# FFN up-projection of a streaming encoder layer: 16 block products per weight tile against seven, with stored weight operands

## The reference

```python
D_MODEL = 1024; SEQ = 2048; DEC_SEQ = 64; D_FF = 2816; FFN_CONV = 3

def causal_dwconv(x, prev, w, b):          # one row for each position
    xp = jnp.concatenate([prev.astype(x.dtype), x], axis=1)
    y = b.astype(x.dtype) + w[0] * xp[:, 0:L]
    for j in range(1, k_width):
        y = y + w[j] * xp[:, j:j + L]
    return y, xp[:, L:]

# in trunk_layer, x being (positions, 1024) and ffn_w_in (1024, 5632)
up, ffn_conv_state = causal_dwconv(x @ ffn_w_in, ffn_conv_prev, ffn_conv_w, ffn_conv_b)
gate, val = split_cols(up, (D_FF, D_FF))
x = layer_norm(DN_ALPHA * x + (jax.nn.silu(gate) * val) @ ffn_w_out, ln2_g, ln2_b)
```

## Time and profile before

| | |
|---|---|
| runs | 2884.21 us median of three (2882.98, 2884.21, 2893.74) |
| span of the profiled execution | 2884.9 us |
| stage `ffn_up` in it | from 1303.4 us to 2351.4 us, 1048 us |
| PE busy over the span | 2676.0 us (93%), 14830 matmuls |
| DVE busy | 1303.1 us (45%) |
| ACT busy | 835.6 us (29%) |
| POOL busy | 321.3 us (11%) |
| DMA | 283.7 MB, mean 98 GB/s |

### The profile page before, as it was taken

How to read it: one execution, slowest core, us unless ns; L and a number is a source line. 1 busy time by engine, 2 the same in 40 slices (tenths; PEclk the granted TensorE clock), 3 DMA queues, 4 the chain that set the end, 5 groups by cost and what they waited for, 6 DMA issues and landing times. The chain is left out here.

```text
span 2884.9 us, 43107 instructions
## 1 busy us (share of the span) xinstructions
PE 2676.0 (93%) x14830; PEld 2441.9 (85%) x14830; DVE 1303.1 (45%) x2763; ACT 835.6 (29%) x1585; POOL 321.3 (11%) x351
## 2 busy tenths in 40 slices
PE   6999799948997969997999999999999979999998
PEld 5887799947986858877999999999999968888885
DVE  5342554525775857665333333333333334333323
ACT  4543322215652232224222222222222223111111
POOL 0000100001001740110111111111111100000000
PEclk9999899978997979998999999999999989999999
DMA  5443632158433554435111111111111135232321
GB/s 194 148 148 107 205 113 92 62 60 184 113 101 85 179 179 147 167 120 175 47 45 45 58 36 53 39 50 42 47 44 44 45 124 172 79 92 76 93 78 50
DMA packets 281406, 283.73 MB, mean 98 GB/s; under 512 B 35708, under 2 KB 248836, under 8 KB 281306
## 3 DMA queue, kind: packets, MB, share of 16 engines
q1 hardware_dynamic: 267866, 233.88, 27.3%
q0 software_dynamic: 13456, 48.76, 5.1%
HBM read 174.06 MB, written 109.46 MB: 98 GB/s over the span
## 5 line engine op out<-in xcount | busy, mean ns | idle before, releaser
L99 PE MATMUL fu_ps_y<-fu_xt_hi,fu_w_hi 128*128 128x426 f32 (+1 forms) x1760 | 626.1, 356 | 10.8 <-DVE fu_xt_lo L1926 8.2
L101 PE MATMUL fu_ps_y<-fu_xt_hi,fu_w_lo 128*128 128x426 f32 (+1 forms) x1760 | 626.8, 356 | 0.0
L100 PE MATMUL fu_ps_y<-fu_xt_lo,fu_w_hi 128*128 128x426 f32 (+1 forms) x1760 | 625.9, 356 | 0.0
L99 PEld LDWEIGHTS fu_ps_y<-fu_xt_hi,fu_w_hi 128*128 128x128 f32 x1760 | 331.7, 188 | 21.5 <-issue 11.7
L1960 DVE SCALAR_TENSOR_TENSOR fu_conv<-fu_ps_y,fu_vecs,fu_conv 128x424 f32<-128x424 f32 (+1 forms) x220 | 141.4, 643 | 458.8 <-ACT fu_conv L1897 458.8
L100 PEld LDWEIGHTS fu_ps_y<-fu_xt_lo,fu_w_hi 128*128 128x128 f32 x1760 | 332.0, 189 | 10.2
L101 PEld LDWEIGHTS fu_ps_y<-fu_xt_hi,fu_w_lo 128*128 128x128 f32 x1760 | 331.2, 188 | 9.0
L99 PE MATMUL fd_ps_y<-fd_w_hi,fd_h_hi 128*128 128x512 f32 (+1 forms) x748 | 292.7, 391 | 14.4 <-DVE fd_h_lo L2159 14.3
L100 PE MATMUL fd_ps_y<-fd_w_lo,fd_h_hi 128*128 128x512 f32 (+1 forms) x748 | 292.0, 390 | 0.0
L101 PE MATMUL fd_ps_y<-fd_w_hi,fd_h_lo 128*128 128x512 f32 (+1 forms) x748 | 291.8, 390 | 0.0
L1897 ACT ACTIVATE fu_conv<-fu_ps_y,fu_vecs 128x424 f32<-128x424 f32 (+1 forms) x220 | 153.3, 697 | 426.8 <-PE fu_ps_y L101 346.6
(11 more groups left out here) (281 smaller groups left out, 4177.2 us busy)
## 6 DMA issues: line engine op xcount, KB each, us to landing
fu_w_raw<-ffn_w_in SPq DMA_DIRECT2D x44, 512.0 KB, 4.4
fd_h_raw<-h_t SPq DMA_DIRECT2D x176, 128.0 KB, 2.1
h_t<-fu_h SPq DMA_DIRECT2D x88, 212.0 KB, 2.0
fd_raw<-ffn_w_out SPq DMA_DIRECT2D x22, 512.0 KB, 4.5
x_rows<-pr_xr SPq DMA_DIRECT2D x16, 512.0 KB, 2.8
xt<-pr_xt SPq DMA_DIRECT2D x16, 512.0 KB, 4.0
mo_mx<-mixed SPq DMA_DIRECT2D x16, 512.0 KB, 4.4
mo_x<-x_rows SPq DMA_DIRECT2D x16, 512.0 KB, 3.3
```

The lines of the kernel that those rows point to most:

```text
L99: pe.matmul(out, lhs_hi, rhs_hi, start=first, stop=False)
L100: pe.matmul(out, lhs_hi, rhs_lo, start=False, stop=False)
L101: return pe.matmul(out, lhs_lo, rhs_hi, start=False, stop=last)
```

## The change

`ffn_up` is rewritten; nothing else is, but for two helpers of `Place` that let two tiles lie on the same SBUF bytes (`w_sum` lies on the `lo` half of the split weights `w`, so that a sum is overwritten by its own rest).

The matrix product of gate and value features (two tiles of 128) with 1024 input features (two halves of 512) and two blocks of positions is a 2 x 2 by 2 x 2 block product. It was eight block products of 4 feature tiles x 3 passes; it is now seven (the form of Strassen and Winograd): four sums of weight blocks S1..S4, four differences of activation blocks T1..T4, seven products, and additions of products, some by letting TensorE accumulate onto a bank, some by copies and additions of VectorE and ScalarE. With A11, A12 the gate's weights (first and second half of the input features), A21, A22 the value's, B11, B21 the first block of positions, B12, B22 the second:

```diff
 def ffn_up(nc, d):
...
+        ORDER = (1, 2, 6, 5, 7, 3, 4)
+        CHUNK_OF = (0, 0, 1, 1, 2, 2, 3)
...
+        w_split = nc.dram_tensor("fu_w_split", (KF, 7, P, 2 * KH * P), F32, kind="Internal").ap()
...
             @block.sync
+                def body(q, j, p):
+                    nxt2 = ahead(q, j, 2)
+                    last_two = isinstance(j, int) and j >= KF - 2
+                    if q == 0 and not last_two:
+                        sp.wait_ge(w_lo_done, 4 * j + 4)
+                        sp.wait_ge(s_done, 4 * j + 4)
+                        alone(sp)
+                        load_raw(*nxt2, p)
+                    if q == 0 and last_two:
+                        sp.wait_ge(w_stored[p], 64 * (KF // 2))
+                    for i in range(7):
+                        if i == (2 if q else 0) and not is_first(q, j):
+                            store_h(*before(q, j))
+                        if q == 0 and i < 4 and not (isinstance(j, int) and j == KF - 1):
+                            store_w(j + 1, 1 - p, i)
+                        if nxt2 and nxt2[0] >= 1:
+                            load_w(*nxt2, p, i)
+                    if isinstance(j, int) and j == 1 and q + 1 < NQ:
+                        sp.wait_ge(x_lo_done, 7 * (q + 1))
+                        load_x(q + 1)
             @block.gpsimd
-                        pool.tensor_tensor(h[:, g % 2, :n], conv[:, v % 2, :n], gate[:, g, :n], ALU.mult).then_inc(h_done, 1)
             @block.scalar
+                split_hi(0, 0, 0)
+                for slot in range(2):
+                    split_x_hi(0, slot)
+                split_hi(0, 0, 1)
...
+                split_x_hi(0, 6)
                 act.wait_ge(vec_turned, 1)
+                act.copy(vecs[:].rearrange("p a b -> p (a b)"), ps_v[:, 0:6 * MT]).then_inc(vec_done, 1)
             @block.vector
+                def body(q, j, p):
+                    if not is_first(q, j):
+                        taps(*b, 3, gate1[:, :nb], c12)
+                        taps(*b, 4, val0[:, :nb], ps_a[:, 1 - p])
+                    if turn:
+                        for step in differences(dve, q + 1)[2:]:
+                            step()
...
+                    if split:
+                        sums(nxt[1], 1 - p, (0,))
+                        split_lo(nxt[1], 1 - p, 0)
+                    if not is_first(q, j):
+                        products_h(*before(q, j), 1 - p)
+                    dve.wait_ge(mm_done, 7 * u + 2)
+                    dve.wait_ge(copy_done, 3 * u + 1)
+                    dve.tensor_tensor(c11[:, :w], p1[:, :w], ps_b[:, p, :w], ALU.add).then_inc(add_done, 1)
...
+                    taps(q, j, 1, gate0[:, p, :n], c11)
...
+                    dve.tensor_tensor(c22[:, :w], p5[:, :w], ps_a[:, p, :w], ALU.add).then_inc(add_done, 1)
...
+                    dve.tensor_tensor(c12[:, :w], u2[:, :w], ps_c[:, p, :w], ALU.add).then_inc(add_done, 1)
...
+                    taps(q, j, 2, val1[:, :n], c22)
+                    if split:
+                        split_lo(nxt[1], 1 - p, 3)
+                    if turn:
+                        for slot in range(3, 7):
+                            split_x_lo(q + 1, slot)
             @block.tensor
                 pe.wait_ge(vec_done, 1)
+                def body(q, j, p):
+                    u = KF * q + j
+                    wait_if(pe, conv_done, 4 * (u - 2) + 4)
+                    product(q, j, p, 1, ps_a, True)
+                    wait_if(pe, add_done, 3 * (u - 2) + 1)
+                    product(q, j, p, 2, ps_b, True)
+                    pe.wait_ge(copy_done, 3 * u + 1)
+                    product(q, j, p, 6, ps_a, False)
+                    product(q, j, p, 5, ps_c, True)
+                    pe.wait_ge(copy_done, 3 * u + 2)
+                    product(q, j, p, 7, ps_a, False)
+                    pe.wait_ge(copy_done, 3 * u + 3)
+                    product(q, j, p, 3, ps_c, False)
+                    pe.wait_ge(add_done, 3 * u + 2)
+                    product(q, j, p, 4, ps_a, False)
```

More of the change, by code:

```diff
@@ L1726, in ffn_up @@
[L1726 to L1733, removed]
[L1734 removed]
+        vec_loaded, vec_turned, vec_done = m.sem("vec_loaded"), m.sem("vec_turned"), m.sem("vec_done")
@@ L1824, in _ @@
+                units(sp, body)
+                store_h(NQ - 1, KF - 1)
+                for p in range(2):
+                    sp.wait_ge(w_stored[p], 64 * (KF // 2))
+                sp.wait_ge(h_stored[0], 16 * NU)
+                sp.wait_ge(h_stored[1], stored1(NU, NQ - 1))
                 sp.wait_ge(states_done, 2)
@@ new lines, in tap0, with tap0_c21 @@
+                def tap0(q, j, which, out, src):
+                    n = width(q)
+                    mt = j + KF * (which in (1, 3))
+                    alone(act)
+                    act.activation(out, src[:, 0:n], ACT.Identity, bias=one(vecs[:, 3, :], mt), scale=one(vecs[:, 0, :], mt)).then_inc(tap0_done, 1)
+                def tap0_c21(q, j):
+                    u = KF * q + j
+                    act.wait_ge(mm_done, 7 * u + 7)
+                    wait_if(act, h_stored[0], 16 * u)
+                    tap0(q, j, 3, val0[:, :width(q)], ps_a[:, parity(j)])
@@ L1996, in _, with product @@
-                pairs(pe, step)
-                pe.wait_ge(conv_done, U * KF)
+                def product(q, j, p, which, bank, first):
+                    slot = SLOT[which]
+                    n = H + width(q)
+                    if q == 0:
+                        pe.wait_ge(w_lo_done, 4 * j + CHUNK_OF[slot] + 1)
+                    else:
+                        pe.wait_ge(w_loaded[p][slot], 8 * (KF * (q - 1) + j - p) + 16)
+                    if isinstance(j, int) and j == 0:
+                        pe.wait_ge(x_lo_done, 7 * q + slot + 1)
+                    out = bank[:, p, :n]
+                    for k in range(KH):
+                        wh, wl, xh, xl = w_hi[:, p, slot, k, :], w_lo[:, p, slot, k, :], x_hi[:, slot, k, :n], x_lo[:, slot, k, :n]
+                        pe.matmul(out, wh, xh, start=first and k == 0, stop=False, skip_group_check=True)
+                        pe.matmul(out, wh, xl, start=False, stop=False, skip_group_check=True)
+                        last = pe.matmul(out, wl, xh, start=False, stop=k == KH - 1, skip_group_check=True)
+                    last.then_inc(mm_done, 1)
```

557 lines of the change are left out of this document (361 added, 196 removed).

## The result

The changed kernel takes 2810.0 us (median of four runs, 2807.9 to 2813.6) against 2884.3: ratio 0.974, interval 0.9722 to 0.9758. A second set of runs gave 2813.9 and 0.9754 (0.9732 to 0.9776). The forecast was 2806, the range 2775 to 2855. The profiled execution has a span of 2810.0 us against 2884.9.

A forecast was written before the change was run, and what follows sets the result against it. TensorE alone was taken to bound the ffn_up stage. Terms 27 + 319 + 301 + 303 + 11 + 8 = 969 us against 1048, 79 less, gave 2806 us, range 2775 to 2855.

The forecast's parts named there:

- TensorE's pace: In ffn_up, a matmul costs its columns plus 13 to 17 ns; TensorE's work falls from 1026 to 905 us.
- A unit of q = 0: Three nearly full queues wait for one another, so a unit takes 14.5 us (13.7 to 15.2), 319 us for 22.
- TensorE's own pace in q = 0: Rival: full overlap on VectorE, q = 0 at 13.7 us a unit, 301 us; 2781 us in all; chance 0.15.
- the rival that they bind q = 0: DMA engines set q = 0: 15.4 us a unit, 2820 to 2865 us, chance 0.22; no change (2887), 0.05.
- The rival of slower weight loads in q = 1 and 2: TensorE's first product of a unit waits for a late load; at 260 GB/s slower than before; chance 0.08.
- SyncE's queue, taken at nothing: In q = 0, raw loads are never late and store_h stands ahead of store_w, so the queue costs 0 us.
- Turns: Between q's, single-buffered activation operands make TensorE stand 3 to 4 us each turn, 3 more ending q = 0: 11 (5 to 18).
- The clock, taken at nothing: TensorE stays at 2.4 GHz through short waits, 0 us; some 2 us each if a turn brings it to 1.2 GHz.
- Start and end: First matmul at 27 us (25 to 30) against 12.2, after ScalarE's casts and vector copy; end 8 us instead of 9.3.
- POOL's absence gives nothing: GpSimd's products hid behind TensorE before, so taking them off GpSimd gains 0 us.

The follow-up runs named there:

- the last run: Kernel with C11 ahead of the products and activations on GpSimd's queue, now moving only 512 of 4096 bytes per split-weight row: 2784.7 us, ratio 0.9641.

## Why the prediction was right, and where it was not

Steady pace and stalls, beside the sum's terms (us; the forecast's 11 for turns is put to the stalls):

```
                       forecast   measured
start                      27       28.25
q=0 steady, 22 units      319      314.0   (22 x 14.27)
q=1 steady                301      301.0   (22 x 13.68)
q=2 steady                303      300.2   (22 x 13.647)
stalls beside these        11       23.6
end                         8        8.65
stage                     969      975.7
```

**TensorE's pace**: right. 163 ns was said for 354 columns and 164 for 356; 162.9 were measured for 354 and 162.5 for 356, 14 to 15 ns above the columns, as in the earlier trace rows. By the Trainium skill's rule for an isolated gap (page "TensorE: Matmul & The Clock Gate", section "Back-to-back issue gap"), 2.5 ns above the columns, one estimates 150 ns for 354; it isn't seen here either. This term carries the result.

**A unit of q = 0**: right in size (14.5 said, 14.27 measured, VectorE's instructions within 0.01 us of the rows), half right in its reason. The text held that three full queues can't work without waiting for one another, and gave TensorE's own pace in q = 0 a chance of 0.15. The run with C11 first shows TensorE without a wait, VectorE busy 96% and the DMA engines full, in one window of 200 us. The order printed in the change had the wait in it: tap 0 behind C11, C11 behind two products. The text put a total on the waits instead of asking which instruction could be moved.

**The DMA engines**: the rival that they bind q = 0 got 0.22 and 0.05. For the steady unit it is refuted: 14.27 us at 356, at 131 and at 99 GB/s. 371 GB/s were held for 200 us with stores and loads mixed, which the rows before couldn't show; the forecast counted four windows of them at 376 to 401 GB/s, where its rows have three and a fourth at 288. The Trainium skill's 358 per core (page "DMA: Bandwidth & Descriptors", section Specifications) is passed. Its page "HBM Reference", section Specifications (TRN2), calls 358 the share with the other core of the pair at work and gives a core alone some 425. The trace, of a kernel on one core, agrees in that 358 is passed; no window of 200 us here shows more than 374. In the unsteady units the rival was in part right, which the text hadn't weighed apart: the last run puts 12.8 us of q = 0 to them, in the kernel with VectorE's order mended. The rival of slower weight loads in q = 1 and 2 is refuted: 13.68 us a unit at 296 GB/s, though at a DMA share of 0.89 and not the 0.75 forecast, which had been worked out from a window of one microsecond.

**SyncE's queue, taken at nothing**: this step failed. It was argued for raw loads and for `store_h` ahead of `store_w`, each issue 0.4 us. The 2.9 MB of activations in unit 1 were left out of it, and issues that full DMA engines hold for 4 to 6 us. It is the unit of 21.4 us, 7.1 above its neighbours, and in q = 1 1.9 net (18.2 and 11.1 against 2 x 13.7). For the first, the run with the activations elsewhere shows it (13.8 for 21.3). Of the 7.1 us TensorE stands 4.33; 1.3 more are the clock, below.

**Turns**: 11 us said, 12.0 measured, counted by TensorE's own starts. From the first matmul of a unit to that of the next, units 20, 21 and 22 take 17.06, 14.67 and 20.32 us, 9.8 above two units of 14.27 and one of 13.68; the first unit of q = 2 takes 15.81, 2.2 above its neighbours. The C11 intervals show less, 6.5 and 2.1 (105.9 against 97.5 us, less the 1.9 just named, and 84.1 against 82.0), because a C11 starts 7.4 to 7.7 us behind its unit's first matmul in steady q = 0 and 4.2 in q = 1. The size was right, the split was not: 3 to 4 us were said for each turn and 3 for the end of q = 0, and TensorE stands 3.81 us behind the first turn, 0.92 behind the second, and 2.44 and 0.72 ahead of the first.

**The clock, taken at nothing**: this step failed too. The text had seen that a wait of 1 us leaves the clock where it is, named "some 2 us each" should the turns bring it down, and put nothing into the sum. Three times TensorE starts again at a granted clock of 0.50, which is 1.2 GHz: at the first matmul of the stage (after 11.70 us without one), in the unit of 21.4 us (after 4.33) and behind the first turn (after 3.81). Windows in these places (columns as in the earlier trace rows):

```profile
1331.00:1336.00 5.00, 5.00 (x18) 5.00 (x18) 4.97 (x6) 1.40 (x2) 0.00 (x0) 0.50 0.80 267
1384.00:1387.00 3.00, 3.00 (x10) 3.00 (x11) 2.89 (x6) 1.43 (x2) 0.00 (x0) 0.50 1.04 422
1665.00:1670.00 5.00, 5.00 (x18) 5.00 (x19) 4.93 (x9) 0.95 (x2) 0.21 (x4) 0.50 0.73 292
```

Matmuls are 0.295 us apart there instead of 0.163. Some 18, 10 and 18 of them are, which is 2.4, 1.3 and 2.4 us, 6 us in all. In the 20 us from 1660 TensorE did 84 matmuls where 123 fit, 6.4 us short, but was idle for 3.8; the other 2.6 are the clock.

**The stalls summed**: the 23.6 us are 7.1 + 1.9 of late stores, 12.0 of turns, 2.4 in the first three units (unit 0 takes 16.41 us from matmul to matmul, 2.7 above TensorE's pace, with no wait of 0.3 us or more in it: the slower clock), and 0.2 at the last matmul. The sum had nothing for the first three units: it took the start to be over with the first matmul.

**Start and end**: 28.25 and 8.65 against 27 and 8. The step said that ScalarE's copy of the vectors, behind all casts, sets the start. The trace of waits says so too (11.70 us for `fu_vecs`), and the run that moved it gained next to nothing: TensorE then stands 5.69 us in unit 0 for ScalarE's copy of P1, which comes behind the same casts, and the first C11 comes behind all of VectorE's splits, 35.6 us after the stage's first issue where 35.8 stood. The value was right, the releaser named was only the last of two.

**POOL's absence gives nothing**: incomplete. Products on GpSimd would free VectorE of 1.05 us a unit and cost it 1.15, so it is GpSimd without arithmetic that lets VectorE's other instructions have the lengths of the rows. The sum was right only because the change had moved the products.

So the 4 us of error in the total are larger ones that cancel: 7.8 us fewer in the steady units, 12.6 more in stalls (9.0 of them late stores), and 2 more at the edges, less 2.6 outside the stage. TensorE's pace, which carries the gain, was forecast; that the total came within 4 us is in part luck.

## What to carry to other kernels

When several engines fit a period with a few per cent to spare, look at the order of instructions on the fullest one before doubting the fit: moving one addition ahead of two products was worth 0.6 us in each steady unit, 11 us in q = 0. Write down what stands in a DMA queue ahead of every store whose buffer is single, bulk loads that are issued once included, and keep bulk loads out of the stretch in which the DMA engines are full. Where TensorE will stand for several microseconds, put the slower matmuls behind the wait into the sum as well as the wait. An engine's wait names the last releaser only; whether a step is worth moving is settled by what the other chains do until then.
